# A masking pass moved from the matrix engine to the vector engine in three attention stages of a two-block transformer kernel

## The reference, cut to what matters

```python
# SWA: 4 groups of 4 query heads, 4 blocks of 128 queries, window of 256 keys
s = jnp.where(valid[None, :, None, None], s, -jnp.inf)
m = jnp.maximum(jnp.max(s, axis=-1, keepdims=True), sink)
p = jnp.exp(s - m)
denom = jnp.sum(p, axis=-1, keepdims=True) + jnp.exp(sink - m)
o = jnp.einsum('bnkgij,bnjkd->bnikgd', p / denom, vb)
o = o.reshape(b, L, ATT_WIDTH) * jax.nn.silu(gate.astype(f32))
# DA: 8 heads with two maps each, causal, 528 tokens
p = jax.nn.softmax(s, axis=-1)
a = p[:, :, 0] - lam * p[:, :, 1]
# DSA: 8 pairs of heads; only the top 128 keys of an index score take part
s = jnp.where(valid[:, None], s, -jnp.inf)
p = jax.nn.softmax(s, axis=-1)
```

## Time and profile before

| | us |
|---|---|
| median of 3 runs | 2490.12 (2489.03 to 2490.16) |
| the profiled execution | 2486.38 |
| its span, first to last instruction | 2484.3 |
| SWA, products and attention | 543 to 784 |
| DA, products and attention | 868 to 1143 |
| DSA, attention | 1757 to 2022 |

### The profile page before, as it was taken

The page is one execution under the profiler, slowest core; times in us unless marked ns, Lnnn a source line. Parts: engine busy times, 40 slices in busy tenths (PEclk is TensorE's granted clock), DMA queues, the critical chain, the costliest instruction groups (busy, mean ns, idle before and its releaser), DMA issues. The chain is left out here.

```text
span 2484.3 us, 41025 instructions
## 1 busy us (share of the span) xinstructions
PE 2250.7 (91%) x15376; PEld 1952.1 (79%) x15376; DVE 1452.3 (58%) x2528; ACT 1014.6 (41%) x1847; POOL 75.5 (3%) x43
## 2 busy tenths in 40 slices
PE   5999995979986799998999999988888879999998
PEld 4777773847664598876999999967766659999997
DVE  6778787354443646665566653379654445666532
ACT  4555544234443345544434432323344434434322
POOL 0000000000000000000000000112111000000000
PEclk8999997989997899997999999988999979999998
DMA  4533320343201111111332333311111113332321
GB/s 116 146 102 101 101 76 21 98 76 77 60 9 32 54 51 51 51 34 51 86 93 85 92 105 90 77 35 30 42 32 34 34 34 86 92 92 85 110 85 43
DMA packets 361091, 172.06 MB, mean 69 GB/s; under 512 B 67519, under 2 KB 359128, under 8 KB 361000
## 3 DMA queue, kind: packets, MB, share of 16 engines
q1 hardware_dynamic: 360616, 170.28, 25.1%
q0 software_dynamic: 384, 0.58, 0.2%
HBM read 168.68 MB, written 2.16 MB: 69 GB/s over the span
## 5 line engine op out<-in xcount | busy, mean ns | idle before, releaser
L274 PE MATMUL ps<-h_parts,parts 128*128 128x264 f32 (+1 forms) x8672 | 1335.6, 312 | 28.8 <-DVE h_parts L298 16.4
L274 PEld LDWEIGHTS ps<-h_parts,parts 128*128 128x128 f32 x8672 | 1195.6, 190 | 127.0 <-issue 30.9
L233 ACT ACTIVATE parts<-ring 128x1024 fp32r<-128x1024 f32 (+1 forms) x286 | 311.0, 1092 | 738.4 <-PE ps L274 506.7
L249 DVE TENSOR_TENSOR parts<-ring,parts 128x1024 fp32r<-128x1024 f32 (+1 forms) x257 | 325.5, 1271 | 247.9 <-ACT parts L233 247.6
L274 PE MATMUL ps<-wide_parts,parts 128*128 128x264 f32 (+1 forms) x1152 | 350.9, 305 | 0.0
L274 PE MATMUL ps<-up_hidden,parts 128*128 128x264 f32 x1408 | 257.8, 285 | 1.8 <-PEq L2149 1.8
L274 PEld LDWEIGHTS ps<-wide_parts,parts 128*128 128x128 f32 x1152 | 219.5, 191 | 8.0
L274 PEld LDWEIGHTS ps<-up_hidden,parts 128*128 128x128 f32 x1408 | 217.9, 188 | 2.1 <-issue 2.1
L2132 DVE TENSOR_TENSOR up_u<-ps,norm_rstd 128x264 f32<-128x264 f32 x176 | 75.3, 429 | 162.7 <-PE ps L274 155.3
L241 POOL TENSOR_TENSOR parts<-ring,parts 128x1024 fp32r<-128x1024 f32 x29 | 69.5, 2399 | 1860.5 <-ACT parts L233 1860.5
L1577 PE MATMUL ps<-wide 64*128 64x256 f32 (+5 forms) x384 | 76.0, 481 | 24.2 <-ACT wide L1714 16.8
(11 more groups left out here) (293 smaller groups left out, 2470.2 us busy)
## 6 DMA issues: line engine op xcount, KB each, us to landing
ring<-in_ffn_w_up SPq DMA_DIRECT2D x88, 512.0 KB, 3.8
ring<-in_ssm_w_in SPq DMA_DIRECT2D x48, 512.0 KB, 4.1
ring<-in_ffn_w_down SPq DMA_DIRECT2D x32, 704.0 KB, 4.5
ring<-in_att_w_in SPq DMA_DIRECT2D x48, 256.0 KB, 3.6
ring<-in_da_w_qkv SPq DMA_DIRECT2D x24, 512.0 KB, 3.8
ring<-in_dsa_w_in SPq DMA_DIRECT2D x24, 512.0 KB, 3.7
ssm_prefix<-prefix_rows SPq DMA_DIRECT2D x32, 256.0 KB, 4.1
ring<-in_ssm_w_out SPq DMA_DIRECT2D x16, 512.0 KB, 4.2
```

The source lines that it names most:

```text
L233: self.nc.scalar.activation(self.part(st, u, 0), self.slot(u, st.kt), ACT.Copy).then_inc(self.w_high, 1)
L249: self.nc.vector.tensor_tensor(self.part(st, u, 1), self.slot(u, st.kt), self.part(st, u, 0).bitcast(F32), ALU.subtract).then_inc(self.w_l ...
L274: m = self.nc.tensor.matmul(out, w[:, n], b, start=start and f == j == 0, stop=stop and f == st.kt - 1 and j == 2)
```

## The change

1. In SWA, DA and DSA no mask goes through PE. DVE reads the scores from PSUM, adds the mask from SBUF (bf16), writes the sum to `p` in SBUF and gives out its maximum, all in one `tensor_tensor_reduce` per head or map. ACT's Exp then reads `p` and writes it back in place. In DA a sheet of zeros and the causal block, built once, serves as mask (`sheet`).
2. The score buffer is free once DVE has read it: `scores(n + 1)` waits for `masked`, no longer for `exp`.
3. The small operations are done per map (DA, DSA) or per half of two heads (SWA), so that the second half's mask pass stands beside the first half's Exp.
4. In SWA the pieces move by two places: the gate pieces of group s are computed at the start of the attention of group s itself.
5. In DSA `pv(2)` no longer waits for Exp of tile 3, and `pv(3)` waits for `masked` of tile 4 instead of `pn`. All but the first three low parts go from POOL to DVE.
6. The feed-forward net's semaphores are shared by its two uses, with counts that go on (`past`).

```diff
 # swa
-                        pe.wait_ge(sem["exp"], 16 * s + 4 * n)
+                        pe.wait_ge(sem["masked"], 16 * s + 4 * n)
-                    for b in range(2):
-                        nc.tensor.matmul(S[:, 2 * b:2 * b + 2, k0:2 * P], k.identb[:],
-                                         k.maskb[:, k0:2 * P].unsqueeze(1).to_broadcast([P, 2, 2 * P - k0]), start=True, stop=False)
+                        if q < 2:
+                            piece(s, 4 + q)
+                        elif not last:
+                            piece(s + 1, q - 2)
-                        do(v.reduce_max(mx[:], S[:, :, k0:2 * P], AX.X))
-                        do(v.scalar_tensor_tensor(nm[:], mx[:], -0.125, nsg[:], ALU.mult, ALU.min))
-                        v.tensor_tensor(es[:], nm[:], nsg[:], ALU.subtract).then_inc(sem["nm"], 1)
+                        for y in range(2):
+                            z = slice(2 * y, 2 * y + 2)
+                            for r in (2 * y, 2 * y + 1):
+                                v.tensor_tensor_reduce(p[:, r, k0:2 * P], S[:, r, k0:2 * P], k.maskb[:, k0:2 * P], 1.0, -3e38, ALU.add, ALU.max,
+                                                       accum_out=mx[:, r:r + 1]).then_inc(sem["masked"], 1)
+                            dve.wait_ge(sem["masked"], 16 * s + 4 * n + 2 * y + 2)
+                            do(v.scalar_tensor_tensor(nm[:, z], mx[:, z], -0.125, nsg[:, z], ALU.mult, ALU.min))
+                            v.tensor_tensor(es[:, z], nm[:, z], nsg[:, z], ALU.subtract).then_inc(sem["nm"], 1)
 # pairs
-                    elif n < 4 or diff:
-                        pe.wait_ge(sem["exp"], 10 * s + 2 * n)
+                    else:
+                        pe.wait_ge(sem["masked"], 10 * s + 2 * n)
+                        if n == 4 and not diff:
+                            pe.wait_ge(sem["o"], 5 * s + 3)
-                        for x in range(2 if masked else 0):
-                            mask = k.maskb[0:nq, P:P + nq] if diff else mb[0:nq, n, lo:hi]
-                            m = nc.tensor.matmul(S[0:nq, x, at:hi], k.identb[0:nq, 0:nq], mask, start=False, stop=True)
-                    if n == 2 and not diff:
-                        pe.wait_ge(sem["exp"], 10 * s + 8)
                     if n == 3 and not diff:
-                        pe.wait_ge(sem["pn"], 5 * s + 5)
+                        pe.wait_ge(sem["masked"], 10 * s + 10)
+                        for j, x in enumerate(MAPS):
+                            v.tensor_tensor_reduce(p[0:nq, x, 0:N], S[0:nq, x, 0:N], mask(n), 1.0, -3e38, ALU.add, ALU.max,
+                                                   accum_out=mx[0:nq, x:x + 1]).then_inc(sem["masked"], 1)
+                            dve.wait_ge(sem["masked"], 10 * s + 2 * n + j + 1)
+                            v.tensor_scalar(nm[0:nq, x:x + 1], mx[0:nq, x:x + 1], -0.125, None, ALU.mult).then_inc(sem["nm"], 1)
+                        if not diff and n == 2:
+                            k.low_on_vector(dve, st, st.after(s + 1, 0, st.depth))
+                        for j, x in enumerate(MAPS):
+                            dve.wait_ge(sem["exp"], 10 * s + 2 * n + j + 1)
+                            do(v.reciprocal(rd[0:nq, x:x + 1], den[0:nq, x:x + 1]))
```

More of the change, by code:

```diff
@@ L160, in __init__ @@
         self.granted = self.sem("refills_granted")
+        self.passed = self.sem("waits_passed")
+        self.up_sem = {x: self.sem("up_" + x) for x in ("done", "free", "tap", "conv", "silu", "out", "zero", "conv_middle")}
         self.w_high, self.w_low = self.sem("weights_high"), self.sem("weights_low")
@@ L1334, in pv, with step @@
                     m.then_inc(sem["pv"], 1)
-                def step(i, lin=True, att=True):
-                    s = i - 1
+                def step(s, last=False):
                     for q in range(6):
[L1339 to L1355, removed]
-                pre.pe(pe)
[L1357 to L1361, removed]
+                        if q == 0:
+                            rot(s, 0), rot(s, 1)
+                        if q == 1:
+                            rot(s, 2), vtr(s)
+                        if q == 2:
+                            scores(s, 0)
+                        if q == 3:
+                            trans(s, 0), scores(s, 1)
+                        if q == 4:
+                            pv(s, 0), trans(s, 1), scores(s, 2)
+                        if q == 5:
+                            pv(s, 1), trans(s, 2), scores(s, 3)
+                        if q < 2:
+                            piece(s, 4 + q)
+                        elif not last:
+                            piece(s + 1, q - 2)
+                    pv(s, 2), trans(s, 3), pv(s, 3)
+                pre.pe(pe)
+                for q in range(4):
+                    piece(0, q)
+                step(0)
+                with pe.Fori(1, KV - 1) as s:
+                    step(s)
+                step(KV - 1, last=True)
             @block.scalar
@@ L2106, in ffn_up @@
     u = k.sb(name + "_u", [P, 4, 2 + T2], F32, ctx)
-    s_done, s_free, s_tap, s_conv, s_silu, s_out = (k.sem(f"{name}_{x}") for x in ("done", "free", "tap", "conv", "silu", "out"))
-    first = k.sem(name + "_zero")
-    s_mid = k.sem(name + "_conv_middle")
-    last = st.iterations - 1
+    s_done, s_free, s_tap, s_conv, s_silu, s_out = (k.up_sem[x] for x in ("done", "free", "tap", "conv", "silu", "out"))
+    first, s_mid = k.up_sem["zero"], k.up_sem["conv_middle"]
+    last, past = st.iterations - 1, l * st.iterations
     def tile(x, t):
```

175 lines of the change are left out of this document (89 added, 86 removed).

## The result

The changed kernel takes 2417.86 us (median of 4 runs, 2417.53 to 2419.17) against 2490.14 us, a ratio of 0.9705 (95% interval 0.9689 to 0.9722). The forecast was 2436 us, range 2420 to 2466. The profiled execution took 2417.98 us, its span 2415.9, so the two profiles differ by 68.4 us.

What follows compares the result with a forecast made beforehand. PE was taken to bound the kernel: by work in DA, waits in DSA, waits and low clock in SWA's last group. DSA 35 + DA 7 + SWA 13.3 = 55.3, less about 1: 54 us; 2436 us, range 2420 to 2466.

Steps and rivals of the forecast that it cites:

- The three limits: Middle DA head: PE work alone; middle DSA head: 5.0 us of PE waits; SWA's last group: waits and low clock.
- the half-rate rival: The mask pass's elements run at half rate on DVE, 0.29 us more per 256; 2469 us, chance 0.07.
- the slower rival: Each pass costs x us above 0.10; DSA loses 72 x; kernel slower from x = 0.61; chance 0.05.
- these terms: SWA: masks 9.0, gate pieces in rotary waits 2.6, Silu no longer ahead of a copy 1.7; 13.3 us.
- the walk: Link-by-link pricing of the new order: middle DSA head 28.2 us; SWA's scaled-tile waits counted as zero change.
- 25.9 + 2.3 = 28.2 us: Middle DSA head: PE work without masks plus waits; 4.3 us less than now, 25.8 us for six heads.
- the 25.9 us of PE: Middle DSA head: PE's need without a wait, 27.47 us busy less 1.6 us of masks.
- more than the sum: DSA and SWA's last group: fewer waits keep the clock up, 14 us more; 2422 us, chance 0.20.
- 6.5: DSA's last head: us saved by shorter links before the last transposes and at the tiles, with the masks.
- the median of the runs shown is 3.7 us above it: Whole kernel: profiled execution would take 2432 us, so the median was put at 2436.
- the stall: DSA: POOL's 2.37 us pass held a DVE negation for 1.67 instead of 0.17 us; 1.5 us in each of six heads.

Runs made afterwards that it cites:

- x1: Kernel before without DSA's mask matmuls; 2478.3 us, 14.4 under the kernel before of its group (ratio 0.9933).
- x7: Changed kernel with every mask pass of DSA done twice into the same place; 2465.8 us (+48).
- x4: Changed kernel with DSA's two low parts a head moved on DVE, behind the cosine products and behind the scaling of tile 3; 2413.8 us (-4.0).
- x3: Changed kernel with DSA's old waits of scores and pv put back; 2433.6 us (+15.7).
- x12: Changed kernel with DSA's old waits and with its small operations for both maps together again; 2452.4 us (+34.5).
- x10: Changed kernel with DSA's mask matmuls issued as well, so the mask is added twice; 2428.0 us (+10).
- b1: Kernel before, unchanged, profiled once more; 2496.6 us.
- b2: Kernel before, unchanged, another extra profile; 2497.3 us.
- b3: Kernel before, unchanged, another extra profile; 2489.2 us.
- x9: Kernel before with DSA's low parts on DVE in the changed kernel's places; 2489.8 us, ratio 0.9981 to the kernel before.
- x2: Changed kernel with all of DSA's low parts on POOL again; 2417.6 us (0).
- x5: Changed kernel with SWA's scores(n + 1) issued ahead of trans(n) and pv(n - 1); 2408.5 us (-9.3).
- x8: Changed kernel with DSA's low parts moved, SWA's scores(n + 1) ahead of trans(n), and v copied ahead of gate piece 5's eviction; 2393.5 us (-24.3).
- x11: Changed kernel with the old SWA whole; median 2438.9 us (+21).
- b4: Changed kernel with the old SWA, profiled once more; 2434.5 us.
- x6: Changed kernel with DSA's small operations for both maps together again; 2429.1 us (+11.3).

## Why the prediction was right or wrong

**What holds.** The three limits were read rightly. The pass costs what its kin in the earlier trace rows cost, so neither the half-rate rival nor the slower one had a case. The Trainium skill's half-rate rule (Vector Engine (DVE) Microarchitecture Reference, Points that are easy to get wrong) speaks of two non-bf16 sources in SBUF; a pass with one source in PSUM and a bf16 mask is not slowed in this trace, 687 ns for 512 elements. Where its letter does apply, the trace does not show the halving either: a `scalar_tensor_tensor` of 528 elements with two fp32 sources in SBUF, which gives out no accumulator, takes 769 ns, and the measurement decides. DA gave 6.4 us against 7, its heads some 0.4 us each against 0.5; no experiment takes DA's part alone. The masks in DSA are 1.51 us a head in x1 against 1.6. The mechanism of the slower rival is real, its factor too high: a head of x7 pays 5.0 of 7.3 us, 0.69 where the rival had 0.9, and its 48 us come near the 52 of the rival's sum only with the 7 us of lower clock.

**Near by luck in part.** SWA gave 14.6 against 13.3, but not by these terms alone. PE's waits for the scaled softmax, which the walk left as they were, fell from 17.7 to 14.3 us. `scores(0)` of the last group waited 0.96 us for v, not 2.0. Against that, the third group has 1.5 us at the lower clock (53.2 instead of 51.7 us) in the changed kernel's profile.

**The step that failed: "25.9 + 2.3 = 28.2 us".** It is 25.5 + 1.2 = 26.75 us. Of the 2.3 us of new waits, the walk had 0.6 at `trans(0)`, 0.9 at `trans(2)`, 0.2 at the scores of tile 1 and 0.6 for the rotation; measured are 0.41, 0.27, none and 0.53. The largest error is `trans(2)`: the walk put the low part on the chain as a link of its own. It stands from 1879.53 to 1880.75, and both Exp end beside it at 1880.3 us, so only the last 0.4 us were late. And the 25.9 us of PE were taken from a head with waits. Without masks, PE's busy time in a head goes with its waits. Heads of x4, x3 and x12, with 0.53, 2.6 and 4.4 us of waits:

```profile
1862.60:1888.53 25.93, 25.40 (x220) 20.47 (x220) 18.34 (x58) 14.41 (x40) 0.00 (x0) 1.00 0.15 40
1839.21:1867.51 28.30, 25.66 (x221) 20.46 (x219) 18.24 (x58) 14.47 (x40) 0.00 (x0) 1.00 0.14 37
1882.52:1912.89 30.37, 25.88 (x218) 20.52 (x218) 16.63 (x48) 14.50 (x39) 0.00 (x0) 1.00 0.12 35
```

With masks it hardly does: 27.41 us with 0.5 us of waits (x10) and 27.47 with 5.0. So a price for the masks that is taken beside waits (1.6) is too low where the waits are gone (1.9); why, no run shows. Against the forecast that is 0.4 us in the first head, 1.7 in the second, 1.4 in each of the next four and 2.0 in the seventh, 9.9 us.

**A second part of the same term: the clock.** The walk priced the head at the upper level, and the six heads were multiplied from it. But the earlier trace rows's head was an undisturbed one; the head shown above, 1778.97 to 1814.15, took 35.2 us, 2.7 more, and the changed kernel has no such head. The rival "more than the sum" named the clock for DSA as a whole and for SWA's last group; the sum itself had nothing for it. With these 2.7 us and 2.4 more in the last head (8.9 against 6.5; no run takes that apart), the 15 us are accounted for.

**A second step that failed: "the median of the runs shown is 3.7 us above it".** I carried these 3.7 us over. The changed kernel's profile is at its median (2417.98 and 2417.86). That is the other 3.9 of the 18 us by which the gain exceeds the forecast; the steps above are the 14.4 us between the profiles. The distance was not a constant of the measurement: executions of the kernel before differ by stretches at the lower clock. b1 and b2, at 2497 us, have them in DSA's heads and in SWA; b3, at 2489.2 the nearest to the runs of 2490, has them in SWA alone (third group 55.7 instead of 54.1 us, fourth 46.8 instead of 45.0). Where the runs of 2490 themselves had them was not profiled. The changed kernel's four runs lie within 1.6 us.

**What the change consists of.** From the two ends, a middle head's 5.75 us are: masks 1.51 (x1), low parts off POOL 1.03 (x9), waits and halves together 3.62 (x12), which makes 6.16; 0.4 us overlap. The prediction gave the waits and the stall a common bill of 2.7 us. Which part "did it" depends on what is there already: moving the low parts is worth 1.0 us a head as the only change (x9) and nothing when the other parts are there (x2).

## What to carry to other kernels

Walk the new order link by link, but lay each added instruction beside the one that it would run with: an instruction inserted where its engine waits for another costs only what sticks out. When a change takes away PE's waits, look for stretches of the old trace in which the same work takes longer at a lower clock, and count them as a possible gain; one profile may show few of them, so compare the profiled execution with all timed ones first. And once a buffer is released earlier, look at the program order around it: here SWA's order of `scores` and `trans`, kept from the old release, cost 9 us with the new one (x5).

## What the runs showed of the hardware

- Whether a middle head of DSA ran in part at the lower clock went with the longest wait of PE in it. With waits up to 0.4 us (after, x4, x5, x8, x10, x11, b4), or 0.8 us (x2, x3), none of the six distances behind the first head was longer than its kin; with 1.3 to 1.7 us, it was one of six (before, b3, x9, x12), two (x1), four (x7) or five (b1, b2); x6, with 0.9 us, had one. That the waits cause it is inferred from these counts, most of them from one profile a kernel, and from where the rows change; it is not shown by itself. Equal waits do not give equal counts (before and b1: 1.6 us, one and five).
- A POOL pass of 2.37 us held some DVE instructions until it ended, and left others alone. Held were the negation of two elements before (1.67 instead of 0.17 us, ending at 1864.02, POOL at 1863.99) and the scaling of 256 elements in x2 (1.60 instead of 0.35 us, ending at 1877.06, POOL at 1876.91). Under the same passes the maxima and mask passes out of PSUM (0.42 and 0.41 us), the one-element negations (0.15) and the reciprocals (0.17) kept their time.
- Giving out DVE's accumulator takes 83 ns, less than half of ACT's 196.
